# Output weights split behind the projection, norms passed on by tile, and the experts' fourth weight buffer loaded with the other three

## The reference

```python
def first_block(x, ...):
    for l in range(2):
        h = _mixing(x, w_in[l], ..., w_out[l])            # 4 kinds of attention heads
        x = _layernorm(alpha * x + h, ln1_g[l], ln1_b[l])
        m = _hier_moe(x, w_group[l], ..., w1[l], w3[l], w2[l])   # 16 experts, 2 per token
        x = _layernorm(alpha * x + m, ln2_g[l], ln2_b[l])
    return x
```

## Time and profile before

| | us |
|---|---|
| median of 3 executions (2544.62 to 2551.57) | 2547.86 |
| the profiled execution | 2550.69 |
| its span, first to last instruction | 2548.9 |
| PE busy | 2228.6 |
| DVE busy | 1156.9 |
| ACT busy | 809.5 |
| POOL busy | 234.0 |

### The profile page before, as it was taken

The page is one execution under the profiler, slowest core; times in us unless marked ns, Lnnn a source line. Parts: engine busy times, 40 slices in busy tenths (PEclk is TensorE's granted clock), DMA queues, the critical chain, the costliest instruction groups (busy, mean ns, idle before and its releaser), DMA issues.

```text
span 2548.9 us, 29583 instructions
## 1 busy us (share of the span) xinstructions
PE 2228.6 (87%) x10942; PEld 1535.1 (60%) x10942; DVE 1156.9 (45%) x1587; ACT 809.5 (32%) x1057; POOL 234.0 (9%) x263
## 2 busy tenths in 40 slices
PE   5898759999498876999949989979989989898998
PEld 4575443443367544343427877768867868776787
DVE  2644460000465445100045555465565566667455
ACT  2333220001133321100013433534433335494333
POOL 4000011110000001132110000010010010001000
PEclk9988879999798887999969998889989989898999
DMA  9737629998463673999955545345545545324553
GB/s 177 240 99 259 227 97 398 416 411 350 154 236 116 231 253 132 370 414 414 418 196 166 189 140 174 101 156 187 188 151 181 181 135 180 117 87 137 174 189 116
DMA packets 213824, 545.14 MB, mean 214 GB/s; under 512 B 25085, under 2 KB 40541, under 8 KB 188225
## 3 DMA queue, kind: packets, MB, share of 16 engines
q1 hardware_dynamic: 187456, 507.74, 55.5%
q0 software_dynamic: 18320, 22.55, 3.6%
q10 hardware_dynamic: 7920, 13.18, 1.4%
HBM read 611.92 MB, written 13.25 MB: 245 GB/s over the span
## 4 chain that ended last, share of the span: by engine, by line
issue 43%; PE 19%; DVE 3%; DMA 3%; POOL 2%; ACT 1%; POOLq 1%; DVEq 1%; ACTq 0%; SPq 0%
PE ps L1284 4%; PE ps L1307 2%; PE ps L512 2%; PE ps L513 2%; PE ps L514 2%; PE ps L1320 2%; POOL rs L2423 1%; PE ps L1269 1%; PE ps L995 1%; PE ps L1342 1%; DMA proj<-in_w 1%; POOLq L2422 1%; DVE w_lo L490 1%; DMA ring<-in_w_out 0%; ACT w_hi L483 0%
## 5 line engine op out<-in xcount | busy, mean ns | idle before, releaser
L490 DVE TENSOR_TENSOR w_lo<-ring,w_hi 128x2048 fp32r<-128x2048 f32 (+4 forms) x232 | 502.7, 2168 | 512.3 <-ACT w_hi L483 491.3
L483 ACT CAST w_hi<-ring 128x2048 fp32r<-128x2048 f32 (+4 forms) x232 | 418.9, 1807 | 721.2 <-PE ps L514 629.4
L512 PE MATMUL ps<-w_hi,XTh 128*128 128x512 f32 (+4 forms) x1328 | 524.8, 395 | 22.0 <-DVE w_lo L490 9.1
L513 PE MATMUL ps<-w_lo,XTh 128*128 128x512 f32 (+4 forms) x1328 | 515.7, 388 | 0.0
L514 PE MATMUL ps<-w_hi,XTl 128*128 128x512 f32 (+4 forms) x1328 | 515.1, 388 | 0.0
L512 PEld LDWEIGHTS ps<-w_hi,XTh 128*128 128x128 f32 x1328 | 259.1, 195 | 88.3 <-issue 16.5
L514 PEld LDWEIGHTS ps<-w_hi,XTl 128*128 128x128 f32 x1328 | 257.8, 194 | 52.1
L513 PEld LDWEIGHTS ps<-w_lo,XTh 128*128 128x128 f32 x1328 | 259.1, 195 | 48.4
L512 PE MATMUL ps<-w_hi,hTh 128*128 128x512 f32 x320 | 125.0, 391 | 0.0
L514 PE MATMUL ps<-w_hi,hTl 128*128 128x512 f32 x320 | 124.7, 390 | 0.0
L513 PE MATMUL ps<-w_lo,hTh 128*128 128x512 f32 x320 | 124.6, 389 | 0.0
(11 more groups left out here) (522 smaller groups left out, 2993.8 us busy)
## 6 DMA issues: line engine op xcount, KB each, us to landing
moe_w<-in_w SPq DMA_DIRECT2D x144, 1024.0 KB, 10.7
ring<-in_ffn_w SPq DMA_DIRECT2D x128, 1024.0 KB, 5.1
ring<-in_ada_w SPq DMA_DIRECT2D x72, 1024.0 KB, 6.0
proj<-in_w SPq DMA_DIRECT2D x48, 1024.0 KB, 10.8
ring<-in_w_in SPq DMA_DIRECT2D x24, 1024.0 KB, 6.8
ring<-in_mb_w_in SPq DMA_DIRECT2D x20, 1024.0 KB, 5.2
ring<-in_ml_w_in SPq DMA_DIRECT2D x12, 1024.0 KB, 5.2
ring<-in_w_out SPq DMA_DIRECT2D x8, 1024.0 KB, 6.0
```

The source lines that it names most:

```text
L483: nc.scalar.copy(w_hi[:, i, 0:n], ring[:, j, 0:n]).then_inc(hi_ready, 1)
L490: nc.vector.tensor_tensor(w_lo[:, i, 0:n], ring[:, j, 0:n], w_hi[:, i, 0:n].bitcast(F32), ALU.subtract).then_inc(raw_used, 1)
L512: nc.tensor.matmul(out, sh, mh, start=start, stop=False)
L513: nc.tensor.matmul(out, sh, ml, start=False, stop=False)
```

## The change

Three things are done in the first block.

**Output weights.** The two `w_out` pieces (0, 0) and (1, 0) go to the head of `RING`, right behind the pieces of the projection. `project_move` splits them ahead with the projection's last unit (`more=2`), and the splits at `SPLIT_AT` are gone. Heads 0 and 1 take no `ada` piece (`ADA_HEAD`). Pieces 26 and 27, which stood in the heads loop, stand between units 0 and 1 of the finish, and unit 1 now stands ahead of `turn_out_tensor(3)`. The early heads are summed behind i = 9 as before (`SUM_AT`), and weighed behind i = 13 (`WEIGH_AT`) rather than 10.

**Norms by tile.** Statistics are taken a tile at a time, in the second norm while the other tile's rows are still on their way. `Y` and `X` are written tile by tile, and `dve_did` counts each. The transposes go tile by tile over four banks (`X_BANKS`), and the products of the first projection piece wait for their own group alone (`x_arrived`). The first two weight pieces of the next layer, or of the second block, are split ahead: both on ACT and one on DVE before DVE adds the experts' rows, once POOL has issued the four row fetches (`rows_asked`), and the second on DVE behind the transposed X.

**Fourth buffer.** `Xh` moves into `feat` and `Xl` into `Y`, so that buffer 3 is free when the other three are, and its load follows theirs at once.

```diff
-        Xh = at("Xh", [P, NT, KD, P], F32R, proj_at + 4 * 4096)
-        Xl = at("Xl", [P, NT, KD, P], F32R, proj_at + 4 * 6144)
+        Xh = at("Xh", [P, NT, KD, P], F32R, feat_at + 4 * 4096)
+        Xl = at("Xl", [P, NT, KD, P], F32R, Y_at)
...
+        def normed_vector(dve, t, tt):
+
+            if tt == 0:
+                dve.wait_ge(row_ready, t.row.at(2))
+            last = nc.vector.scalar_tensor_tensor(Y[:, tt, :], Y[:, tt, :], mv[:, tt, 0:1], LN_GAIN,
+                                                  ALU.subtract, ALU.mult)
...
+            if tt == 0:
+                root_arrived(dve, t)
+            last = nc.vector.scalar_tensor_tensor(X[:, tt, :], Y[:, tt, :], rs[:, 2, tt:tt + 1], LN_SHIFT,
+                                                  ALU.mult, ALU.add)
...
+            t.add(dve_step=1)
             dve.drain().then_inc(dve_did, 1)
...
+        X_BANKS, TURNED_ORDER = (2, 3, 6, 7), (0, 2, 1, 3)
+
+        def turn_x_tensor(pe, t):
+            for g in range(4):
+                tt, b0 = g // 2, 4 * (g % 2)
+                if g % 2 == 0:
+                    pe.wait_ge(dve_did, t.dve_step.at(tt - 1))
+                for i in range(4):
+                    last = nc.tensor.transpose(ps[:, X_BANKS[g], i * P:(i + 1) * P],
+                                               X[:, tt, (b0 + i) * P:(b0 + i + 1) * P], ident[:, :])
+                last.then_inc(turned, 1)
+                t.add(turn=1)
...
-        RING = (list(range(8, 25)) + [(0, 0), 25, (1, 0), 26, 27, 28, (0, 1), 29, 30, 31, (1, 1), 32, 33, 34, 35])
+        RING = [(0, 0), (1, 0)] + list(range(8, 28)) + [(0, 1), 28, 29, 30, 31, (1, 1), 32, 33, 34, 35]
+
+        ADA_HEAD = 2
...
-                if u == 3:
-                    sp.wait_ge(gather_act, t.gathered.at(12))
-                    sp.wait_ge(gather_dve, t.gathered.at(12))
-                elif u > 3:
+                if u > 3:
...
+            pool.sem_inc(rows_asked, 1)
             root_pool(pool, NT)
...
+            dve.wait_ge(rows_asked, t.block.at(0, 1, N_BLOCKS))
+            split_ahead(dve, t, split_vector)
...
+            for tt in range(NT):
+                both_rows(tt)
+                means_vector(dve, tt)
+            for tt in range(NT):
+                normed_vector(dve, t, tt)
...
-            project_move(dve, t, split_vector, 1, W_IN, take_in(1), behind=behind, single={UQ: 768, UKV: 512},
+            turn_x_vector(dve, t)
+            split_vector(dve, t)
+            project_move(dve, t, split_vector, 1, W_IN, take_in(1), behind=behind, more=2, single={UQ: 768, UKV: 512},
                          beyond=[u + 2 for u in ADA_UNITS])
...
-        TURN_AT, SQUARE_AT, SPLIT_AT = (17, 18, 19), 8, (16, 17)
+        TURN_AT, SQUARE_AT, SUM_AT, WEIGH_AT = (17, 18, 19), 8, 9, 13
...
-                ada_in_ring(pe, t, ADA_FIRST + i)
+                if i >= ADA_HEAD:
+                    ada_in_ring(pe, t, ADA_FIRST + i - ADA_HEAD)
...
             unit(0)
-            ada_in_ring(pe, t, 28)
+            for i in (26, 27):
+                ada_in_ring(pe, t, i)
+            unit(1)
             pe.wait_ge(dve_did, t.dve_step.at(4))
             turn_out_tensor(pe, t, 3)
-            unit(1)
-            for i in (29, 30, 31):
+            for i in range(28, 32):
                 ada_in_ring(pe, t, i)
```

More of the change, by code:

```diff
@@ L817, in layer_norm_vector @@
             dve.drain()
             nc.vector.tensor_scalar(rs[:, 0, 0:NT], mv[:, :, 1], 1e-5, None, ALU.add).then_inc(mean_ready, 1)
-            dve.wait_ge(row_ready, t.row.at(2))
-            for tt in range(NT):
-                last = nc.vector.scalar_tensor_tensor(Y[:, tt, :], Y[:, tt, :], mv[:, tt, 0:1], LN_GAIN,
-                                                      ALU.subtract, ALU.mult)
-            last.then_inc(row_used, 1)
-            dve.drain()
-            root_arrived(dve, t)
@@ L831, in layer_norm_vector @@
             dve.drain().then_inc(dve_did, 1)
         def layer_norm_scalar(act, t):
-            t.add(row=2, dve_step=1, root=1)
+            t.add(row=2, dve_step=2, root=1)
         def layer_norm_tensor(pe, t, layer, g):
@@ L838, in layer_norm_tensor, with turn_x_scalar, turn_x_vector, x_arrived @@
             row_tensor(pe, t, layer, g + 1, 4)
-            t.add(dve_step=1, root=1)
-        def x_transpose_tensor(pe, t, buf):
-            pe.wait_ge(dve_did, t.dve_step.at())
-            turn_tensor(pe, t, x_groups(buf)[0])
+            t.add(dve_step=2, root=1)
+        X_BANKS, TURNED_ORDER = (2, 3, 6, 7), (0, 2, 1, 3)
[9 more added lines that the diff above has]
+                t.add(turn=1)
+        def turn_x_scalar(act, t):
+            for g in range(4):
+                tt, b0 = g // 2, 4 * (g % 2)
+                act.wait_ge(turned, t.turn.at(1))
+                nc.scalar.copy(XTh[:, b0:b0 + 4, tt * P:(tt + 1) * P],
+                               ps[:, X_BANKS[g], :].rearrange("p (b s) -> p b s", s=P)).then_inc(turned_hi, 1)
+                t.add(turn=1)
+        def turn_x_vector(dve, t):
+            for g in TURNED_ORDER:
+                tt, b0 = g // 2, 4 * (g % 2)
+                at = (slice(None), slice(b0, b0 + 4), slice(tt * P, (tt + 1) * P))
+                dve.wait_ge(turned_hi, t.turn.at(1 + g))
+                nc.vector.tensor_tensor(XTl[at], ps[:, X_BANKS[g], :].rearrange("p (b s) -> p b s", s=P),
+                                        XTh[at].bitcast(F32), ALU.subtract).then_inc(turned_lo, 1)
+            t.add(turn=4)
+        def x_arrived(pe, t, k, tt):
+            pe.wait_ge(turned_lo, t.turn.at(2 - 3 + 2 * k + tt))
+        def split_ahead(eng, t, split):
+            for _ in range(2 if split is split_scalar else 1):
+                split(eng, t)
         def up_sync(sp, t, w, n):
@@ L1645, in between @@
                     t.add(raw=-1)
-            project_tensor(pe, t, x_lhs, W_IN, behind=behind, between=between,
+            project_tensor(pe, t, x_lhs, W_IN, arrived=x_arrived, behind=behind, between=between,
                            single={UQ: of_latents(0, 2), UKV: of_latents(2, 1)})
```

93 lines of the change are left out of this document (45 added, 48 removed).

## The result

The changed kernel took 2539.03 us, the median of 20 executions (2528.78 to 2546.77), against 2551.48 for 20 of the kernel before. The ratio is 0.9949 (95% interval 0.9938 to 0.9960). It is faster by 12 us, beyond the 0.3% that a measurement can tell, and not by the 42 that were forecast: the time lies above the range of 2490 to 2523.

The account below looks back on a forecast made before the run. Experts are filled by PE's own instructions, so gains lie in each layer's other half, where PE waits. 15.1 us a layer, twice 30.2, plus 12.1 once, from 2550.7, less 2.8, gives 2506 us; range 2490 to 2523.

Parts of the forecast that it names:

- Projection's end: Last projection product into the first heads: scores start 3.1 later, missing ada pieces give about 3.2 back; 0, bounds -3.5 to +0.5.
- Rival C: Heads run at the lower clock: in one layer 2549 us (chance 0.04), in both 2592, slower (0.05).
- Rival A: The delay of 3.1 at the projection's end is not given back and the finish gains nothing: 2519 us, chance 0.20.
- Heads 9 to 12: Heads loop: later weighing removes DVE's wait for POOL's root; 3.2 us a layer gained, bounds 1.5 to 5.
- Heads 16 to 18: Heads loop: w_out splits on ACT and DVE leave; 7.2 us a layer gained, bounds 4.6 to 9.9.
- Finish: Last head turn to the norm's rows: two splits fewer ahead of freed slots; 3 us a layer gained, bounds 0 to 6.
- Norm 1: Norm before the router: order by tile brings the first router product earlier; 1.7 us a layer, bounds 0.5 to 2.5.
- Fourth buffer: Experts' start: earlier load gains 0 in layer 0, about half of PE's wait, 1.5 us, in layer 1; bounds 0 to 5.4.
- no transfer wait of PE in layer 1's experts: Sign expected in the profile after: PE in the second layer's experts no longer waits for a buffer's load.
- rival B: Experts are bound by transfers at their start, so the earlier buffer gains up to 5.1 us a layer: 2497 us, chance 0.09.
- Boundaries: Early weight splits: 7.6 us gained from layer 0 to 1 (bounds 6 to 9), 3 into the second block (2.3 to 4.3).
- a branch's fetch: Layer 0 to 1: DVE's 3.35 us stall at a branch stays unchanged by the edit; without it the kernel would take 2502 to 2503.

Follow-up runs that it names:

- pieces back, split moved: Changed kernel with the second w_out split moved into the heads loop and ada pieces again in heads 0 and 1, so out of the finish: 2517.74 us.
- the held slot: Changed kernel, but DVE's early split at a layer's end leaves its ring slot to be freed by the last sum of the fetched rows: 2534.01 us.
- the finish in another order: Moved split, pieces back and slot held, plus unit 2 between pieces 29 and 30, unit 3 between 33 and 34, last ada addition behind residual sum: 2515.89 us.

## Why the prediction was wrong, point by point

**Projection's end, forecast 0, measured -7.1 and -7.1.** This is the step that failed most. The delay of the scores was put at 3.1; PE's row shows 3.49 of wait, and from the last product to the first score it took 8.0 instead of 3.5, so 4.5. Worse was the payback: "heads 0 and 1 lose their `ada` pieces" was counted as 3.6 gained. It was right that PE sets the pace there, but its clock was taken as given. With 15 products fewer PE was busy 33.7 us up to `use(2)` in layer 0 instead of 30.6, at a clock of 0.69 instead of 0.78. Wait and missing pieces both have a part: with either of them alone the clock's mean is 0.64 to 0.67, with neither 0.78 in most profiles (the table above). The split must leave first, and then the pieces pay for themselves by bringing the clock back. The lower bound of -3.5 priced the delay alone. Rival C named the clock and tied it to the missing pieces, but as an all-or-nothing case of 43 us a layer, where it was a matter of some 10 us more at the lower clock in a layer. Rival A had the wait that moves, at 3.4 instead of 7.

**Heads 9 to 12, forecast 3.2 a layer, measured 0.2 up to `use(16)`.** The prediction put all 6.7 over the pace down to DVE's instructions and its wait. But that stretch ran at a clock of 0.77 before already, with PE busy 10.8 us of it; at 1.00, with the sum and the weighing out, the same stretch keeps PE busy 8.7. The wait for the root went, and the low clock stayed (0.76). The term needed two more facts: that DVE's sum alone makes PE wait 2.28, after which the clock drops, and that the shift by two pieces put the addition of 0.69 next to it. How much each of the two adds is not shown apart.

**Heads 16 to 18, forecast 7.2, measured 7.6 and 8.6.** The splits were the cause: with them back in place (without the part on the output weights) the stretch takes 14.2 and 15.0. But what they cost was half seen. PE's busy time for the same 40 products fell by 4.1, because the clock was 0.55 before and is 1.00 now; the waits fell by 3.5. The prediction had the whole as work of DVE and ACT in a row, so the size is in part luck. Up to the last turn it was 7.6 and 9.3.

**Finish, forecast 3, measured -0.3 and -1.3.** The wait for the late roots is gone, as said. The mis-sized term is the landing, taken at 5.3 to 6.0; in the kernel before it was 5.3 for this piece, issued 3.1 behind the load ahead of it. In the profile after, SP issued the last `w_out` piece at 282.73 and ACT began on it at 290.00, 7.3 later; the load ahead of it had been issued 1.2 before:

```profile
284.44 1.93 PE L1031 MATMUL ps<-ring,mid 128*32 128x512 f32 x8 [1.91 <-DMA ring<-in_ada_w]
287.25 1.93 PE L1031 MATMUL ps<-ring,mid 128*32 128x512 f32 x8 [0.88 <-DMA ring<-in_ada_w]
...
290.00 1.90 ACT L485 CAST w_hi<-ring 128x2048 fp32r<-128x2048 f32 x1 [8.61 <-DMA ring<-in_w_out]
```

And the pieces behind the new wait run at 1.93. PE's busy time in the stage rose from 36.6 to 39.7, of which 2.1 are the two pieces, while its waits fell from 7.2 to 4.4. Without these two pieces (pieces back, split moved) the landing took 9.2 and the stage 43.3, with 6.2 of waits, which fits an end set by what lands rather than by PE's added work. No run had a faster landing to prove it. The estimate of 4.4 us for a landing, worked out from the Trainium skill, DMA: Bandwidth & Descriptors, "Anatomy of one DMA", was further off: the row shows 7.3 with others under way. The page gives that fit for transfers issued by GpSimd, and these are issued by SP.

**Norm 1, forecast 1.7, measured 1.4 and 1.7.** Right. The first router product starts at 325.31, behind a wait of 1.74 for `XTl`.

**Fourth buffer, forecast 1.5, measured 4.6 by its removal and 0.7 by the two traces,** so the size stays open. The sign "no transfer wait of PE in layer 1's experts" did not come: one of 2.20 is left. The place, layer 1 alone, fits, and so does the judgement that rival B would not hold, since layer 0 did not move.

**Boundaries, forecast 7.6 and 3, measured 5.6 and -0.3.** The chain behind X was right: with the held slot the two places take 8.1 and 2.6 less than before, which is near what was forecast. What was left out is that the split frees a slot, and that SP's next load then shares the DMA engines with the row fetch. Following the queue behind the freed slot would have led to it. By the two profiles this cost 2.5 at the first place and 2.9 at the second. The rule of the Trainium skill, Runtime: NRT & Kernel Launch, "Instruction fetch mechanics", on a branch's fetch stayed without effect on the sum, as said: DVE is still idle for 3.25 us at the branch, from 661.31 to the first subtraction at 664.56.

Of the 42.3 forecast, 14.3 went at the projection's end, 7.6 in the finish, 5.9 at heads 9 to 16, and 5.4 at the boundaries; 2.5 more than forecast came at heads 16 to the last turn.

**The range.** The prediction says that the bounds of a layer's terms reach from -5 to +6. Its own bounds add up to -12.0 and +8.8 (below: 3.5, 1.7, 2.6, 3 and 1.2). With two layers that is 24 us on the low side of the gain, and the range allowed 17 for the whole, on the ground that the terms would hardly all fall to one side. Three of the five did, each beyond its own bound: -7.1 against -3.5 at the projection's end, 0.2 against 1.5 at heads 9 to 12, -0.3 and -1.3 against 0 in the finish.

## What to carry to other kernels

Work moved ahead of a waiting engine is priced by that engine's wait and by the clock that it has afterwards: behind a wait of 2.28 an `ada` piece took 1.94 instead of 1.07, and two pieces taken out of a stretch that ran at the lower clock made it longer (33.7 us against 31.4), since the clock stayed low longer. So when a stretch lies over the pace, read its granted clock first: `use(16)` to `use(18)` went from 15.3 us at 0.55 to 7.7 at 1.00, and a good half of the gain was clock. When an early step frees a buffer, follow the queue to the transfer that this starts, and ask what lands at that moment. And in a stage that waits for transfers, look for a reordering that brings a transfer forward: one that only changed what waits for them (the finish in another order) moved the wait from one piece to another.

## What the runs showed of the hardware that was not expected

Behind PE's wait of 3.49 us at 177.45 the granted clock was 0.52 from 178.2 to 184.2, and 0.50 up to 196.2; behind that of 2.28 at 235.48 a piece took 1.45 and the next 1.94; behind one of 1.66 (pieces back, at 243.62) a piece took 1.94, while in the changed kernel a wait of 1.66 at 251.02 was followed by a piece of 1.06. The way back was not the same in each execution: for the same instructions, `use(9)` to `use(12)` took 10.3 or 11.9 us, and the last product to `use(0)` 31.4 or 34.8. POOL's issue of an indirect fetch took 1.64 to 2.15 us beside a DVE subtraction of 2048 elements a partition, and 0.99 otherwise. POOL's signal behind its fetches came at 639.64, 4.5 us before the last of them ended.
